# Eighty added pairs of fp32r products, with 128, 127 and 96 weight columns, between an up- and a down-projection

## The chip, the cores and the metric

The kernel runs on one core of a Trainium2 chip. The metric is the device time of one execution in microseconds (us), as a median of several. The core has five engines with a queue each: TensorE (PE in the profile) multiplies matrices, VectorE (DVE) and ScalarE (ACT) work on elements, GpSimd (POOL) does nearly nothing here, SyncE (SP) issues the loads. They meet at semaphores. A matmul holds one operand, the weights, in TensorE's array and streams the other, the moving operand, past it; the result goes to a bank of PSUM. The profile records two things for each: the load of the weights (LDWEIGHTS, on a row of its own, PEld) and the product (MATMUL).

## What is computed

Two transformer-like blocks on 256 tokens of width 2048, all inputs in float32. The part around the change is the feed-forward stage of the second block's first layer:

```python
def _conv_ffn(xn, w_up, conv_w, conv_b, w_down):
    up = xn @ w_up
    u, g = up[..., :D_FF], up[..., D_FF:]
    g = lax.conv_general_dilated(g, conv_w[:, None, :], ...) + conv_b
    return (jax.nn.silu(g) * u) @ w_down

for layer in range(2):
    ...                                   # attention, of another kind in each layer
    h = h + _conv_ffn(_rmsnorm(h, ffn_norm_g[layer]), ffn_w_up[layer], ...)
```

D_FF is 5632. Ahead of both layers stands a block with a gated recurrence and latent attention.

## The kernel before

**Products in two parts.** The large products are made from fp32r operands, a reduced form of float32. Each operand is split into a high part and a low part, so that a product is high x high + high x low + low x high. `pair` (line 647) makes them: for each of the 16 (or 22) blocks `k` of 128 rows and each of two output tiles `j` it issues two matmuls. The wide one holds 128 columns of the weights' high part and streams 512 columns, the high and the low part of the activations beside each other. The short one holds the low part of the weights and streams 256 columns. So a wide and a short product together, here called a couple (the change's own word for two such products is a pair), stream 768 columns. One call of `pair` over 16 blocks is 64 matmuls. The profile writes f32 for fp32r here as for plain float32; the products of line 647 are fp32r, all others with an f32 in their row are plain float32.

**The stage.** `ffn` runs twice, `ffn(False)` and `ffn(True)`. In it `g` goes over two halves of D_FF. In each half 22 calls of `pair` multiply the stream `xs` (128 partitions x 16 blocks x 512 columns, fp32r) with the weights of the up-projection, and then `residual_product(GROUP, ...)` multiplies the result, `ys` (22 blocks), with the weights of the down-projection in 8 calls of `pair`. In front of the down-projection's last two blocks TensorE waits for the last tiles of `ys` (semaphore `lo_out`), which VectorE finishes after the last up-projection's product.

**The supply of weights.** SyncE loads weights into `raw`, a ring of four slots of four blocks. ScalarE makes the high part in `wr` (line 1204), VectorE the low part (line 1654), TensorE waits for a slot (`unit_split`), and frees it (`unit_used`). So ScalarE, VectorE and the loads can be four slots ahead of TensorE, and no more.

**Banks.** `acc` is two pairs of banks, used in turn by `pair`; VectorE adds the two halves of a result when it reads it out (line 1665). `scores`, `turned`, `mixed` and `sums` are four more banks. `scores` is used by attention alone: in the first layer for the last time by `diff_scores`, after which ScalarE reads it (line 1353); in the second layer from `stick_scores` on. `T.scores_read` counts those reads.

**Addresses.** `xs` begins at 64 bytes past a multiple of 256, `wr` at 160 bytes past one (`MOVING_STEP`, `WEIGHTS_STEP`).

Each engine's order is that of its own code; nothing is moved by a scheduler.

Of the kernel before, what the change touches and what calls it, by code (L numbers as in the profile page):

```python
# [25 lines left out]
P = 128  # L26
TOK = 256
D = 2048
KT = D // P
# [195 lines left out]
def splits(units):  # L225

    return {f"unit_split{s}": units // RING for s in range(RING)}
# [58 lines left out]
def program(nc, t, out, consts):  # L286

    ctx = ExitStack()
    with ctx:
# [7 lines left out]
        def sb(name, shape, dt=F32):  # L297
            return ctx.enter_context(nc.sbuf_tensor(name, [P, *shape], dt))
# [39 lines left out]
        xs = sb("xs", [KT, 2 * TOK], F32R)  # L338
# [57 lines left out]
        scores = ctx.enter_context(nc.psum_tensor("scores", [P, 512], F32))  # L396
# [217 lines left out]
        def _(pe):  # L614
            T = Tallies(sems)
# [3 lines left out]
            def pair(right, blocks=KT, before=None, after=None, acc_wait=True, tokens_out=False):  # L619

                a = acc[pairs[0] % 2]
                if pairs[0] >= 2:
                    pe.wait_ge(*T.acc_read.next())
                else:
                    take(2 * pairs[0], 2 * pairs[0] + 1)
                pairs[0] += 1
                for n, k0 in enumerate(range(0, blocks, UK)):
                    s = units[0] % RING  # L630
                    units[0] += 1
                    pe.wait_ge(*T.unit_split[s].next())
                    for k in range(k0, min(k0 + UK, blocks)):
                        if before:
                            before(k)
                        w, x, first, last = wr[:, s, k - k0, :], right(k), k == 0, k == blocks - 1
                        for j in range(2):
                            cols = slice(j * P, j * P + P)
                            low = slice(256 + j * P, 256 + j * P + P)
                            if tokens_out:  # L640
                                wide = (a[:, j, :], x[:, cols], w)
                                short = (a[:, j, 0:256], x[:, low], w[:, 0:256])
                            else:
                                wide = (a[:, j, :], w[:, cols], x)
                                short = (a[:, j, 0:256], w[:, low], x[:, 0:TOK])
                            for ops in ((short, wide) if last else (wide, short)):
                                mm = pe.matmul(*ops, start=first and ops is wide, stop=last and ops is wide)  # L647
                    mm.then_inc(T.unit_used.sem, 1)
                    if after:
                        after(n)  # L650
# [155 lines left out]
            def take(*banks, read=None):  # L806

                for b in banks:
                    pe.wait_ge(*last_read[b])
                read = read or F.bank_read[banks[0]].next()  # L810
                for b in banks:
                    last_read[b] = read
                return bank(banks[0])
# [95 lines left out]
            for g in range(4):  # L909
                b = GA_BANK[g]  # L910
                take(b, b + 1)
                for u in range(4):
                    w = unit_tiles(one_unit())
                    for k in range(UK):
                        for j in range(2):
                            mm = pe.matmul(bank(b + j)[:, 0:TOK], w[:, k, j * P:(j + 1) * P], xm[:, u * UK + k, :],  # L916
                                           start=u == 0 and k == 0, stop=u == 3 and k == UK - 1)
# [32 lines left out]
            def stream_sums():  # L950

                T.squares_summed.n += KT // 2
                pe.wait_ge(T.squares_summed.sem, T.squares_summed.n)
                sums_bank()
                feature_sums(ssq, ones[:, :], sums[:, 0:TOK]).then_inc(T.sums_ready.sem, 1)
# [134 lines left out]
            residual_product(gates={0: 2, 12: 1, 14: 0}, meanwhile=last_head)  # L1090


            def ffn(last):
                ready = T.lo_out.n
                T.lo_out.n += KT // 2

                def normed_by(k):

                    if k % 2 == 0:
                        pe.wait_ge(T.lo_out.sem, ready + k // 2 + 1)  # L1100

                for g in range(2):
                    if g == 0:
                        pair(lambda k: xs[:, k, :], before=normed_by, after=lambda n: stream_sums() if n == 1 else None)
                        pair(lambda k: xs[:, k, :])
                    with T.turns(pe, GROUP // 2 - (g == 0), **splits(2 * UK), acc_read=2):
                        for e in range(2):
                            pair(lambda k: xs[:, k, :])
                    residual_product(GROUP, stored=g == 1 and last, tiles=1)

            ffn(False)


# [68 lines left out]

            residual_product(gates={0: 2, 12: 1, 14: 0}, meanwhile=last_heads)
            ffn(True)


# [1201 lines left out]
```

## Time and profile before

| | us |
|---|---|
| median of 3 runs | 2795.09 (2794.13 to 2795.55) |
| the profiled execution, whole | 2792.86 |
| its span, first to last instruction | 2791.1 |
| TensorE, busy with products | 2728.8 (98% of the span) |
| TensorE, busy with weight loads | 2374.5 (85%) |
| VectorE | 1983.0 (71%) |
| ScalarE | 1192.8 (43%) |
| DMA queue q1 (weights) | 523.60 MB, 62.1% of 16 engines' span |

Loads of weights overlap products, and the length of a product's record takes in its way through the array, which overlaps the next one. So the busy share of TensorE says that it never stands still, not at which pace it goes; the pace is read from the distance between starts.

### The profile page before, as it was taken

How to read it: one execution, taken by the hardware profiler on the slowest of the kernel's cores; microseconds unless marked ns; L12 is line 12 of the kernel's file. 1: busy time of each engine (PE TensorE's matmuls, PEld its weight loads, DVE VectorE, ACT ScalarE, POOL GpSimd, SP SyncE). 2: the span in 40 equal slices, each digit the busy share in tenths (PEclk: the TensorE clock that was granted, in tenths of full speed). 3: DMA queues.
4: the chain of work that ended last, by engine and by line, in shares of the span. 5: the costliest groups of instructions: out<-in, count | busy, mean ns of one | idle time of the engine just before them, and what ended most of it. 6: DMA issues, size and time to landing. Idle time of an engine off the chain costs nothing.

```text
span 2791.1 us, 43966 instructions
## 1 busy us (share of the span) xinstructions
PE 2728.8 (98%) x15236; PEld 2374.5 (85%) x15236; DVE 1983.0 (71%) x2617; ACT 1192.8 (43%) x1517; POOL 5.7 (0%) x12
## 2 busy tenths in 40 slices
PE   6899999999999999999999999999999999999999
PEld 5787888888878888888888888888888888888888
DVE  6555467777777777766777766588777775677765
ACT  1102444455544444444444443355444444444443
POOL 0000000000000000000000000000000000000000
PEclk9999999999999999999999999999999999999999
DMA  9886665555545666656666666643466666666664
GB/s 299 292 261 203 201 197 189 175 159 159 169 132 186 189 188 193 189 186 191 189 188 180 197 193 190 188 154 125 156 188 193 186 184 193 193 187 187 193 198 147
DMA packets 705761, 528.13 MB, mean 189 GB/s; under 512 B 32205, under 2 KB 694543, under 8 KB 705423
## 3 DMA queue, kind: packets, MB, share of 16 engines
q1 hardware_dynamic: 701728, 523.60, 62.1%
q10 hardware_dynamic: 3951, 3.44, 0.4%
q8 instruction: 51, 0.84, 0.1%
q14 instruction: 31, 0.25, 0.0%
HBM read 523.80 MB, written 2.10 MB: 188 GB/s over the span
## 4 chain that ended last, share of the span: by engine, by line
PE 91%; DVE 5%; issue 1%; ACT 1%; DMA 1%; ACTq 0%; SPq 0%; DVEq 0%
PE acc L647 78%; PE acc L727 2%; PE acc L715 2%; PE acc L916 2%; PE turned L727 1%; PE sums L727 1%; DVE pro_ada L1729 1%; DVE wr L1654 1%; PE sums L1031 1%; PE mixed L837 1%; DMA aring<-in_w_ada 1%; PE sums L655 0%; PE scores L1024 0%; ACT three_L L1589 0%; ACTq L1235 0%
## 5 line engine op out<-in xcount | busy, mean ns | idle before, releaser
L647 PE MATMUL acc<-xs,wr 128*128 128x512 f32 (+1 forms) x7680 | 1352.3, 337 | 0.2 <-DVE wr L1654 0.2
L647 PEld LDWEIGHTS acc<-xs,wr 128*128 128x128 f32 x7680 | 1174.4, 188 | 163.7 <-issue 3.8
L1654 DVE TENSOR_TENSOR wr<-raw,wr 128x1024 fp32r<-128x1024 f32 x832 | 1001.6, 1222 | 363.6 <-ACT wr L1204 351.6
L1204 ACT ACTIVATE wr<-raw 128x1024 fp32r<-128x1024 f32 x832 | 871.8, 1058 | 774.2 <-PE acc L647 767.5
L647 PE MATMUL acc<-ys,wr 128*128 128x512 f32 (+1 forms) x4352 | 762.5, 337 | 6.6 <-DVE ys L1688 6.6
L647 PEld LDWEIGHTS acc<-ys,wr 128*128 128x128 f32 x4352 | 666.5, 188 | 97.6 <-DVE ys L1688 6.4
L647 PE MATMUL acc<-wr,xs 128*128 128x512 f32 (+1 forms) x1024 | 183.3, 337 | 0.0
L647 PEld LDWEIGHTS acc<-wr,xs 128*128 128x128 f32 x1024 | 157.1, 188 | 23.0 <-issue 0.5
L1547 ACT ACTIVATE ffn_cv<-ffn_cv 128x256 f32<-128x256 f32 x88 | 36.9, 419 | 245.2 <-DVE ffn_cv L2241 245.2
L1665 DVE TENSOR_REDUCE ffn_ug<-acc 128x512 f32<-128x1024 f32 x88 | 107.8, 1224 | 39.6 <-PE acc L647 39.6
L1729 DVE SCALAR_TENSOR_TENSOR pro_ada<-aring,small,pro_ada 128x512 f32<-128x512 f32 (+1 forms) x112 | 92.4, 825 | 29.7 <-DMA aring<-in_w_ada 23.0
L1688 DVE TENSOR_TENSOR ys<-tmp,ys 128x256 f32 (+3 forms) x108 | 51.3, 475 | 73.2 <-ACT ys L1210 70.2
L1665 DVE TENSOR_REDUCE S<-acc 128x512 f32<-128x1024 f32 x72 | 87.9, 1220 | 21.3 <-PE acc L647 21.1
L1210 ACT ACTIVATE ys<-tmp 128x256 f32 (+3 forms) x104 | 46.8, 450 | 105.4 <-DVE tmp L2245 101.2
L715 PE MATMUL acc<-xm,w 128*128 128x256 f32 x256 | 64.0, 407 | 7.0 <-DVE xm L1747 6.1
L715 PEld LDWEIGHTS acc<-xm,w 128*128 128x128 f32 x256 | 52.0, 206 | 15.5 <-issue 6.4
L1669 DVE TENSOR_TENSOR ffn_ug<-ffn_ug,rx 128x512 f32<-128x512 f32 x88 | 60.8, 691 | 3.0
L916 PE MATMUL acc<-xm,w 128*128 128x256 f32 x256 | 57.3, 379 | 0.0
L916 PEld LDWEIGHTS acc<-xm,w 128*128 128x128 f32 x256 | 47.7, 190 | 6.0
L1286 ACT ACTIVATE sq<-acc 128x512 f32<-128x512 f32 x2 | 1.1, 594 | 119.6 <-PE scores L717 119.6
L2239 DVE SCALAR_TENSOR_TENSOR ffn_cv<-ffn_ug,vcol,ffn_cv 128x256 f32<-128x256 f32 x88 | 42.6, 484 | 13.2 <-DVE ffn_cv L2236 13.0
L2241 DVE SCALAR_TENSOR_TENSOR ffn_cv<-ffn_ug,vcol,ffn_cv 128x256 f32<-128x256 f32 x88 | 42.6, 485 | 13.0 <-DVE ffn_cv L2239 12.8
(306 smaller groups left out, 1505.2 us busy)
## 6 DMA issues: line engine op xcount, KB each, us to landing
raw<-in_ffn_w_up SPq DMA_DIRECT2D x704, 256.0 KB
raw<-in_ffn_w_down SPq DMA_DIRECT2D x160, 512.0 KB
raw<-in_a_w_qkv SPq DMA_DIRECT2D x96, 512.0 KB
raw<-in_b_w_kv SPq DMA_DIRECT2D x64, 512.0 KB
aring<-in_w_ada SPq DMA_DIRECT2D x96, 256.0 KB, 6.6
w<-in_w_in SPq DMA_DIRECT2D x48, 512.0 KB
raw<-in_w_ada SPq DMA_DIRECT2D x32, 512.0 KB, 5.7
raw<-in_w_out SPq DMA_DIRECT2D x32, 512.0 KB
```

The costliest lines, as they stand in the source:

```text
L647: mm = pe.matmul(*ops, start=first and ops is wide, stop=last and ops is wide)
L715: pe.matmul(bank(c // 2)[:, (c % 2) * TOK:(c % 2 + 1) * TOK], w[:, c * P:(c + 1) * P], xm[:, k, :], start=False, stop=k == KT - 1 and c % ...
L727: mm = pe.matmul(out(j), *here, start=k == 0, stop=k == UK - 1)
L916: mm = pe.matmul(bank(b + j)[:, 0:TOK], w[:, k, j * P:(j + 1) * P], xm[:, u * UK + k, :], start=u == 0 and k == 0, stop=u == 3 and k == UK ...
L1204: f(wr[:, s, :, 0:256], raw[:, s, :].rearrange("p (k n) -> p k n", k=UK), ACT.Copy)\
L1210: f(to[0], to[1], ACT.Copy).then_inc(T.hi_out.sem, 1)
L1654: tt(wr[:, s, :, 256:512], raw[:, s, :].rearrange("p (k n) -> p k n", k=UK), wr[:, s, :, 0:256], ALU.subtract).then_inc(T.unit_split[s].se ...
L1665: dve.tensor_reduce(out_tiles, a[:, 0:tiles, :].rearrange("p t (b c) -> p t c b", b=2), axis=AX_X, op=ALU.add)\
L1669: tt(out_tiles, out_tiles, both(rx), ALU.mult).then_inc(*T.acc_read.one())
L1688: tt(to[:, :, TOK:2 * TOK], src, to[:, :, 0:TOK], ALU.subtract).then_inc(*T.lo_out.one())
L1729: stt(here, aring[:, n % ADA_RING, 0:2 * kn * P], small[:, 8 + r:9 + r], here, ALU.mult, ALU.add)\
L2239: step(stt(cv[e][:, :], UG[e][:, 1, 1:1 + TOK], taps[1], cv[e][:, :], ALU.mult, ALU.add))
```

## The change

A new function `probe_products` is called once, on TensorE, in `ffn(False)` with `g == 0`: behind the 22 calls of the first up-projection and ahead of its down-projection. It waits until ScalarE has read the last `scores` of the first layer's attention, and then issues 160 fp32r matmuls, 80 of 512 and 80 of 256 moving columns, all into `scores`, each beginning a sum anew and ending it. Nobody reads what they leave. Both operands lie in `xs`: the moving one is block `k` from its first column on, the weights are 128, 127 or 96 columns of block `k + 1` from column 24 on, that is 160 bytes past a multiple of 256, as in `wr`. The five groups are:

| group | pairs | weight columns | rows | order of widths |
|---|---|---|---|---|
| A | 16 | 128 | 128 | 512, 256 |
| B | 16 | 127 | 128 | 512, 256 |
| C | 16 | 96 | 128 | 512, 256 |
| D | 16 | 128 | 127 | 512, 256 |
| E | 16 | 127 | 128 | 512, 512, 256, 256 |

```diff
+            def probe_products():
+
+                pe.wait_ge(T.scores_read.sem, T.scores_read.n + 1)
+
+                def once(k, cols, width, rows=P):
+                    pe.matmul(scores[0:cols, 0:width], xs[0:rows, (k + 1) % KT, 24:24 + cols], xs[0:rows, k, 0:width],
+                              start=True, stop=True)
+
+                for k in range(KT):
+                    once(k, P, 512)
+                    once(k, P, 256)
+                for k in range(KT):
+                    once(k, P - 1, 512)
+                    once(k, P - 1, 256)
+                for k in range(KT):
+                    once(k, 96, 512)
+                    once(k, 96, 256)
+                for k in range(KT):
+                    once(k, P, 512, rows=P - 1)
+                    once(k, P, 256, rows=P - 1)
+                for k in range(0, KT, 2):
+                    once(k, P - 1, 512)
+                    once(k + 1, P - 1, 512)
+                    once(k, P - 1, 256)
+                    once(k + 1, P - 1, 256)
+
             def ffn(last):
...
                         for e in range(2):
                             pair(lambda k: xs[:, k, :])
+                    if g == 0 and not last:
+                        probe_products()
                     residual_product(GROUP, stored=g == 1 and last, tiles=1)
```

On TensorE the loop of the up-projection was followed at once by the down-projection. Before:

```order
1834 L647 MATMUL acc<-xs,wr 128x256
1835 L647 MATMUL acc<-xs,wr 128x512
1836 L214 REGISTER_ALU
1837 L214 COMPARE_AND_BRANCH
1838 L647 MATMUL acc<-ys,wr 128x512
1839 L647 MATMUL acc<-ys,wr 128x256
```

Now the added products stand behind the loop's end (an order row gives the result's partitions and columns, so that 127x512 is a product with 127 weight columns):

```order
1835 L647 MATMUL acc<-xs,wr 128x512
1836 L214 REGISTER_ALU
1837 L214 COMPARE_AND_BRANCH
1838 L1098 MATMUL scores<-xs 128x512
1839 L1098 MATMUL scores<-xs 128x256
1840 L1098 MATMUL scores<-xs 128x512
1841 L1098 MATMUL scores<-xs 128x256
```

and the last of them, group E, ahead of the same first product of the down-projection:

```order
1978 L1098 MATMUL scores<-xs 127x512 x2
1979 L1098 MATMUL scores<-xs 127x256 x2
1980 L1098 MATMUL scores<-xs 127x512 x2
1981 L1098 MATMUL scores<-xs 127x256 x2
1982 L647 MATMUL acc<-ys,wr 128x512
1983 L647 MATMUL acc<-ys,wr 128x256
```

No other instruction is added, taken away or moved, on TensorE or on any other engine.

## Rows read from the trace of the kernel before

**Rows 1.** The page: busy time by engine, clock in 40 slices, chain by engine.
```profile
PE 2728.8 (98%) x15236; PEld 2374.5 (85%) x15236; DVE 1983.0 (71%) x2617; ACT 1192.8 (43%) x1517; POOL 5.7 (0%) x12
...
PEclk9999999999999999999999999999999999999999
...
PE 91%; DVE 5%; issue 1%; ACT 1%; DMA 1%; ACTq 0%; SPq 0%; DVEq 0%
```

**Rows 2.** Busy time by stretch: start:end length, then PE, PEld, DVE, ACT, POOL, clock, DMA.
```profile
1100.00:1150.00 50.00, 50.00 (x290) 44.02 (x289) 39.70 (x51) 20.77 (x26) 0.00 (x0) 1.00 0.68 197
1150.00:1200.00 50.00, 50.00 (x291) 44.02 (x289) 32.37 (x34) 22.54 (x24) 0.00 (x0) 1.00 0.60 187
...
1157.00:2791.10 1634.10, 1621.24 (x9357) 1425.43 (x9355) 1173.90 (x1445) 730.82 (x843) 0.00 (x0) 1.00 0.61 182
```

**Rows 3.** In order of time, around the place: start us, length us, engine, instruction, [idle].
```profile
1134.99 1.23 DVE L1665 TENSOR_REDUCE ffn_ug<-acc 128x512 f32<-128x1024 f32 x1 [0.46 <-PE acc L647]
...
1146.09 1.23 DVE L1665 TENSOR_REDUCE ffn_ug<-acc 128x512 f32<-128x1024 f32 x1 [0.45 <-PE acc L647]
...
1156.99 43.40 PE L647 MATMUL acc<-ys,wr 128*128 128x512 f32 x249
...
1157.19 1.23 DVE L1665 TENSOR_REDUCE ffn_ug<-acc 128x512 f32<-128x1024 f32 x1 [0.46 <-PE acc L647]
...
1163.30 0.43 DVE L1688 TENSOR_TENSOR ys<-tmp,ys 128x256 f32 x1 [0.81 <-ACT ys L1210]
```

**Rows 4.** In order of time, TensorE, four short looks at the up-projection.
```profile
999.86 0.51 PE L647 MATMUL acc<-xs,wr 128*128 128x512 f32 x2
...
1000.09 0.51 PE L647 MATMUL acc<-xs,wr 128*128 128x256 f32 x2
...
1000.21 0.51 PE L647 MATMUL acc<-xs,wr 128*128 128x512 f32 x2
...
1000.43 0.51 PE L647 MATMUL acc<-xs,wr 128*128 128x256 f32 x2
```

**Rows 5.** In order of time, TensorE, from the first block's end on.
```profile
399.62 3.62 PE L916 MATMUL acc<-xm,w 128*128 128x256 f32 x16
403.08 0.59 PE L837 MATMUL mixed<-one_pT,one_v 128*128 128x256 f32 x2
...
404.39 1.84 PE L866 MATMUL sums<-ones,gate_sum 128*128 128x1 f32 x16
407.02 89.04 PE L647 MATMUL acc<-ys,wr 128*128 128x512 f32 x512 [0.78 <-DVE ys L1688]
495.89 5.72 PE L647 MATMUL acc<-xs,wr 128*128 128x512 f32 x32
```

**Rows 6.** Groups by line and shape: count, busy us, mean ns of one, idle before.
```profile
L647 PEld LDWEIGHTS acc<-xs,wr 128*128 128x128 f32 x7680 | 1174.4, 188 | 163.7 <-issue 3.8 <-DVE wr L1654 0.5
...
L916 PEld LDWEIGHTS acc<-xm,w 128*128 128x128 f32 x256 | 47.7, 190 | 6.0
...
L1025 PEld LDWEIGHTS scores<-chunkb,identb 128*128 128x128 bf16 x32 | 3.1, 98 | 0.4
```

**Rows 7.** Last reads of scores ahead of the place: count, ns min/median/max, first to last start.
```profile
L1353 ACT ACTIVATION_READ_ACCUMULATOR two_p<-scores,small x4: 192/196/201, 816.3 to 819.7; 128x1 f32 x4
```

**Rows 8.** TensorE's waits, whole span: us in total, times, longest us; three of 18.
```profile
PE acc L647 <- DVE ys L1688: 6.6, 3, 3.4
...
PE mixed L1146 <- DVE three_A L2311: 4.9, 7, 1.7
...
PE turned L990 <- DVE ffn_fin L2100: 2.0, 1, 2.0
```

## The prediction

> **What bounds the kernel now.** I read the page first. TensorE is busy with products for 98% of the span, it makes up 91% of the chain of work that ended last, and its clock is granted in full in every slice [rows 1]; the stretches around the place show 1.00, the 2.4 GHz level [rows 2]. Then I asked for the place itself. In the two stretches of 50 us before and behind the end of the first up-projection TensorE is busy for 50.00 of 50.00 us, while VectorE is busy for 39.70 and 32.37 and ScalarE for 20.77 and 22.54 [rows 2]. The timeline shows the seam: the first product of the down-projection begins at 1156.99 with no idle time noted in front of it [rows 3]. The last tile of `ys` is done at 1163.30 + 0.43 = 1163.7, and the down-projection asks for it only in front of its last two blocks, 20 x 4 products behind its start, that is at 1156.99 + 80 x 0.1734 = 1170.9 (pace: below). So there is no wait at this seam that other work could fill. TensorE's own pace is all that counts here, and work put into its queue lengthens the chain by its whole length.
>
> **The pace of one product.** A call of `pair` is 64 matmuls, and VectorE reads its result when it is done: at 1134.99, 1146.09 and 1157.19 [rows 3]. That is 11.10 us each, so 11.10 / 64 = 173.4 ns for one, 346.9 ns for a wide and a short one. A far longer stretch agrees: 512 products from 407.02 to 495.89, 88.87 / 512 = 173.6 ns [rows 5]; the first quarter of these is written out without a loop, as the added ones are, and shows no gap. The starts tell the two widths apart: 999.86, 1000.09, 1000.21, 1000.43 [rows 4], so about 0.23 us for 512 columns and 0.12 for 256. Streaming alone at 2.4 GHz is 213.3 and 106.7 ns, so either has some 13 ns on top (26.9 ns by the better mean of a couple).
>
> **The weight loads.** There are as many loads as products in the whole trace, 15236 of either [rows 1], so 160 loads come with the 160 products. What does a load cost when nothing hides it? The products of one moving column show it: 16 of them take 1.84 us. The last one's record is 0.25 us long by the column of the row's end, so 15 distances take 1.59 us, 106 ns each [rows 5]. Behind a product of 256 columns, at 120 ns, such a load just disappears. Plain float32 products of 256 columns with as many weights come every (403.08 - 399.62) / 16 = 216 ns [rows 5], as long as 512 columns take to stream (213) and 3 ns: there the load is hidden whole. And is the load of an fp32r product of that kind? Its record is 188 ns long, a float32 one's 190, a bf16 one's 98 [rows 6]. I take it that it is: about 106 ns of loading behind an overhead common to all.
>
> **The change part by part.**
> 1. The wait on `scores_read`. ScalarE read `scores` for the last time at 819.7 + 0.2 [rows 7], 337 us before the place. It costs nothing, whatever the price of a semaphore that has long been passed; and nothing else is queued behind it that could have gone first.
> 2. Groups A and D, 32 pairs with 128 weight columns. Same widths, same starts of the operands within 256 bytes, same kind of operand as in `pair`. 32 x 346.9 ns = 11.1 us. That both operands lie in `xs`, that in D one row is missing, and that all results go to one bank instead of to two in turn, no row shows. A wide and its short product go to the same bank in the kernel too, at this pace, so I put nothing for it; my bound for either is the 13 ns on top of each product, gone or doubled, 160 x 13 ns = 2 us.
> 3. Groups B, C and E, 48 pairs with 127 or 96 weight columns. No row shows a load of fewer than 128 columns. From below: the load costs nothing at all and the 13 ns go with it, as in the float32 row: 96 x (13.4 - 2.7) ns = 1.0 us less. From above: it can't be hidden at all, 106 ns on each of the 64 products with 127 columns and 80 ns (three quarters) on each of the 32 with 96, 6.8 + 2.6 = 9.3 us more. I take the row nearest to it, the 128-column load of the same type: no more columns, no longer load, hidden as before. 48 x 346.9 ns = 16.7 us. The order in E (512, 512, 256, 256) puts a short product behind a short one; a load of 106 ns still fits into 120.
> 4. The other engines. Nothing is added to them. While TensorE is away for 28 us, ScalarE and VectorE fill the four slots of `wr` and SyncE those of `raw`, then they stand. That is lead which TensorE can't turn to time, since it waited for no weights here anyway [rows 2, 3]. The last results of the up-projection and `ys` are finished during the added work instead of during the down-projection; no wait depended on that either.
> 5. What comes later. All of TensorE's idle time behind 1157 is 1634.10 - 1621.24 = 12.9 us [rows 2], in waits for values that follow from its own results [rows 8]: `ys` at the start of later products, the sums of attention, the last transposes. A shift of everything by 28 us moves them along.
>
> The sum: 160 x 173.4 ns = 27.8 us. The profiled execution took 2792.86 us (its span of 2791.1 and 1.8 around it); with the change I expect 2820.6 there. The median of the runs is 2795.09, 2.2 us higher, so that the predicted median is 2795.09 + 27.75 = 2822.8 us, 1.0% more.
>
> **The rivals.**
> - *Narrow loads are of a slower kind.* Full columns might be loaded in a quick way that 127 and 96 columns don't get. What rows show as quick and slow is bf16 and float32, 98 and 190 ns, 92 apart [rows 6]. With that on top a narrow load takes 198 ns at 127 columns and 149 at 96. Behind a wide product (227 ns) it is still hidden, behind a short one (120) it stands out by 78 or 29 ns: 32 x 78 + 16 x 29 ns = 3.0 us more, 2825.8. Against it: the record of an fp32r load looks like the slow kind already. This is the rival that a rule of the Trainium skill speaks for, "TensorE: Matmul & The Clock Gate", Weight-path perf modes: fast weight load is on when there are 128 weights and the type isn't FP32, and reads the columns in four chunks side by side. By that rule with its theoretical factor of four an estimate would be 424 ns for a load of 127 columns and some 21 us more, 2843; the same page's section on LDWEIGHTS gives columns / 1.2 in ns, which is 107 at 128 (the trace agrees, 106), 106 at 127 and 80 at 96, and changes nothing.
> - *Narrow loads aren't hidden.* If the array can take new weights beside a running product only in full width, each narrow load stands in the open: 9.3 us more (step 3), 2832.2. For it: no row shows a narrow load hidden. Against it: the full-width load of either type is hidden in these rows, and a narrower one asks for less.
> - *Narrow products are cheaper.* 1.0 us less (step 3), 2821.8. It can't be told from my forecast by the time, only by the starts.
> - *Not slower.* The added work would have to fill time in which TensorE stands. The place for that is the wait for `ys` in the down-projection behind it, and the waits further on. At the seam the idle time is 0.0; giving back all 12.9 us of later idle time would still leave 14.9 us, so this decides only from 22 us of fillable idle time on, and the trace hasn't that. What is left of it is that the change doesn't do what it says: products whose result nobody reads are left out when the program is loaded, 2795.1. The built program holds all 160.
>
> **How the numbers follow.** My forecast (27.8 us, up or down by the 2 us of step 2) 0.68, cheaper narrow products 0.10, narrow loads of a slower kind 0.07 with 0.04 more for far slower ones (2843), narrow loads not hidden 0.09, not slower 0.02. The range from 2820.5 to 2833.0 leaves out the far slower loads, the last case and the odd ends. A difference of 0.2% (5.6 us) is about what a measurement of this kernel can tell from no change; every case but the last is well above it: slower 0.98, same 0.015, faster 0.005.
>
> **What would show it.** In the profile after: a group of 160 products into `scores`, in one stretch from about 1157 to 1184.7, with no idle time before, in or behind it, and the down-projection's first product at 1184.7. The stretch falls into five of 5.55 us each. If B, C and E are longer than A and D, the narrow load is the cause, and the starts say which way: some 80 ns more behind short products alone (a slower kind), or some 106 behind each (not hidden). If C is shorter than B, the load's length counts, so some of it isn't hidden. If A itself isn't 5.55, the fault is in the common step, the operands' place or the single bank. The forecast is wrong if the stretch isn't 27.8 us long within 2, or if the time behind it (1634 us before) changes by more than 1 us.

## The result, and the profile after

| | before | changed |
|---|---|---|
| median of the first 3 runs, us | 2795.09 (2794.13 to 2795.55) | 2820.67 (2819.98 to 2822.2) |
| the profiled execution, whole | 2792.86 | 2819.98 |
| its span | 2791.1 | 2817.9 |

The ratio is 1.0093, with a 95% interval of 1.007 to 1.0116: slower by 0.9%, by 25.6 us by these medians and by 27.1 us by the two profiled executions. The prediction was 2822.8 with a range of 2820.5 to 2833.0. In the experiments below one execution of the kernel before (5535.56 us) and one of idle9 (12833.07 us) were slow ones, which the ratios leave out.

The timeline of the changed kernel around the seam (start us, length us, engine, instruction, [idle]; the lines of the other engines are 28 higher than before, L1693 for L1665 and so on):

```profile
1156.18 1.22 DVE L1693 TENSOR_REDUCE ffn_ug<-acc 128x512 f32<-128x1024 f32 x1 [0.45 <-PE acc L647]
...
1155.98 28.00 PE L1098 MATMUL scores<-xs 128*128 128x512 f32 x160
...
1162.29 0.43 DVE L1716 TENSOR_TENSOR ys<-tmp,ys 128x256 f32 x1 [0.81 <-ACT ys L1238]
...
1183.82 6.41 PE L647 MATMUL acc<-ys,wr 128*128 128x512 f32 x36
1186.80 1.06 ACT L1232 ACTIVATE wr<-raw 128x1024 fp32r<-128x1024 f32 x1 [24.76 <-PE acc L647]
1187.89 1.23 DVE L1682 TENSOR_TENSOR wr<-raw,wr 128x1024 fp32r<-128x1024 f32 x1 [25.18 <-ACT wr L1232]
```

The 160 products stand in one piece, from 1155.98 to 1183.82, 27.84 us, with no idle time in front, inside or behind. ScalarE and VectorE finish the last tile of `ys` in its first quarter (1162.3 + 0.4), and then stand for 25 us: their four slots are full, and TensorE frees none. That lead is worth nothing later, as the busy time of the stretch behind the seam shows, here of the changed kernel (start:end length, PE, PEld, DVE, ACT, POOL, clock, DMA); the same stretch of before is the last of [rows 2]:

```profile
1183.80:2817.90 1634.10, 1621.27 (x9358) 1425.48 (x9356) 1169.23 (x1437) 729.16 (x840) 0.00 (x0) 1.00 0.61 181
```

1634.1 us in either kernel, with 1621.2 and 1621.3 us of products. Behind the seam nothing has changed to a tenth of a microsecond. Ahead of it the profiled execution of the changed kernel is 1.0 us early (1155.98 for 1156.99 in [rows 3]). That is the net of two differences. In the first block shorter waits (one for `pro_ada` took 3.3 us, 5.9 before) and a shorter stretch at half clock put it 3.1 us ahead (its first product of line 647 begins at 403.93, for 407.02 in [rows 5]), and then its clock was at half for a while where that of before stood at 1.00 (0.50 is the granted clock in this row of stretches):

```profile
404.70:408.10 3.40, 3.40 (x13) 2.92 (x12) 2.64 (x3) 2.66 (x3) 0.00 (x0) 0.50 0.81 250
```

That gave half of the lead back: the next products on `xs` begin at 494.38, for 495.89 before, 1.5 us ahead. These are differences between two executions, and no part of the change is there: 27.84 - 1.01 = 26.8 us is the difference of the spans.

The five groups can be told apart by their first products, each row from a short window of its own:

```profile
1155.98 0.39 PE L1098 MATMUL scores<-xs 128*128 128x512 f32 x1
...
1161.53 0.40 PE L1098 MATMUL scores<-xs 128*127 128x512 f32 x1
...
1167.12 0.39 PE L1098 MATMUL scores<-xs 128*96 128x512 f32 x1
...
1172.67 0.40 PE L1098 MATMUL scores<-xs 127*128 127x512 f32 x1
...
1178.24 0.39 PE L1098 MATMUL scores<-xs 128*127 128x512 f32 x1
...
1183.82 0.39 PE L647 MATMUL acc<-ys,wr 128*128 128x512 f32 x1
```

(128*127 in such a row is rows times columns of the weights.) So group A took 5.55 us, B 5.59, C 5.55, D 5.57 and E 5.58. Forecast were 5.55 for each. No longer run was made of D, so its 0.02 us may be chance. The records of the weight loads in this stretch (count, busy us, mean ns of one) do depend on the number of columns:

```profile
L1098 PEld LDWEIGHTS scores<-xs 128*127 128x127 f32 x64 | 9.8, 187 | 1.5
...
L1098 PEld LDWEIGHTS scores<-xs 128*128 128x128 f32 x32 | 5.0, 188 | 0.7
L1098 PEld LDWEIGHTS scores<-xs 127*128 127x128 f32 x32 | 4.9, 188 | 0.7
L1098 PEld LDWEIGHTS scores<-xs 128*96 128x96 f32 x32 | 4.5, 162 | 1.1
```

32 columns fewer make a load 26 ns shorter, 0.8 ns a column, and a product no faster: the load is hidden. A row fewer (127*128) leaves the record of the load at 188 ns.

### The profile page after: what moved, and what is told of

The parts are those of the page before. It is cut to its first block, busy times and chain, and to the rows that moved or that the text cites. A ratio compares the mean times of both kernels' runs of the same rounds, so it can differ in the third digit from the quotient of the medians.

```text
span 2817.9 us, 44286 instructions
## 1 busy us (share of the span) xinstructions
PE 2757.5 (98%) x15396; PEld 2399.2 (85%) x15396; DVE 1983.7 (70%) x2617; ACT 1193.1 (42%) x1517; POOL 5.7 (0%) x12
## 4 chain that ended last, share of the span: by engine, by line
PE 91%; DVE 5%; issue 1%; DMA 1%; ACT 1%; ACTq 0%; SPq 0%; DVEq 0%
PE acc L647 77%; PE acc L727 2%; PE acc L715 2%; PE acc L916 2%; PE turned L727 1%; PE sums L727 1%; DVE pro_ada L1757 1%; PE scores L1098 1%; DVE wr L1682 1%; PE sums L1031 1%; PE mixed L837 1%; DMA aring<-in_w_ada 0%; PE sums L655 0%; PE scores L1024 0%; ACTq L1263 0%
## 5 line engine op out<-in xcount | busy, mean ns | idle before, releaser
L1693 DVE TENSOR_REDUCE ffn_ug<-acc 128x512 f32<-128x1024 f32 x88 | 107.8, 1224 | 39.5 <-PE acc L647 39.5
L1693 DVE TENSOR_REDUCE S<-acc 128x512 f32<-128x1024 f32 x72 | 87.9, 1220 | 21.3 <-PE acc L647 21.1
L2269 DVE SCALAR_TENSOR_TENSOR ffn_cv<-ffn_ug,vcol,ffn_cv 128x256 f32<-128x256 f32 x88 | 42.7, 485 | 13.0 <-DVE ffn_cv L2267 12.8
```

The costliest lines, as they stand in the source:

```text
L1693: dve.tensor_reduce(out_tiles, a[:, 0:tiles, :].rearrange("p t (b c) -> p t c b", b=2), axis=AX_X, op=ALU.add)\
```

## The experiments

The experiments replace the body of `probe_products`, but for idle9. changed_again, eighty_full, full480, narrow480 and idle9 were executed several times; the others once, and they are read from their traces alone. In all of them the results in `scores` are read by nobody, as in the changed kernel. `mm(k, cols, width)` stands in the diffs for `pe.matmul(scores[0:cols, 0:width], xs[:, (k + 1) % KT, 24:24 + cols], xs[:, k % KT, 0:width], start=True, stop=True)`.

### Is it 27.8 us, and is it linear?

**changed_again** is the changed kernel, no edit. Expected:

> The changed kernel, timed again over five rounds beside the kernel before, since its first median was 25.6 us above and the forecast was 27.8. My theory (160 products at the pace of the kernel's own, 173.4 ns, nothing hidden): 27.8 us more, within 1.0 of it. A rival (some 2 us of the added work lie in idle time or are given back later): 25.6 again.

Measured: 2821.96 us against 2793.63 of before beside it, 28.3 us more, ratio 1.0102 (1.0085 to 1.0118). The rival of 2 us given back falls; 25.6 and 28.3 lie on either side of 27.8, and the medians of before themselves moved by 1.5 us between the two (its seven executions here lie between 2791.63 and 2797.18). In its trace the added products take 27.84 us once more.

**eighty_full**:

```diff
-                for k in range(KT):        # groups A to E
...
+                for k in range(80):
+                    mm(k, 128, 512)
+                    mm(k, 128, 256)
```

> 80 couples (a 512-wide and a 256-wide product) that all have 128 weight columns and 128 rows in place of the five groups. My theory: 80 x 346.9 ns = 27.8 us more than before, the stretch in the trace 27.8 us, so the same as the changed kernel but for its groups B and E, which showed 5.59 us in place of 5.55: 0.1 us less. Rival (narrow loads cost something that the groups' distances in the trace don't show): more than 0.5 us less than the changed kernel.

Measured: 2822.09 us, 28.5 us more, ratio 1.0102 (1.0086 to 1.0119): by the time the same as the changed kernel (0.1 us apart). Whatever the narrow weights cost, it can't be seen in the time of 80 couples. In the traces it can: the stretch is 27.74 us here (1155.63 to 1183.37) and 27.84 in the changed kernel, the 0.1 us that was expected.

**full480** and **narrow480** do it six times as long, with 128 and with 127 columns:

```diff
+                for k in range(480):
+                    mm(k, 128, 512)        # narrow480: 127
+                    mm(k, 128, 256)        # narrow480: 127
```

> 480 couples with 128 weight columns, six times the added work. My theory: 480 x 346.9 ns = 166.5 us more, in line with the 80. Rival (code written out without a loop runs short of instructions, or the engine's clock gives way): over 168. Rival (part of the added work is hidden): the increase isn't six times that of 80 couples, but some 2 us less than six times 27.8.

> 480 couples with 127 weight columns. By the distances of group B in the changed kernel (5.589 us for 16 couples against 5.551) 480 couples take 167.7 us where 128 columns take 166.5: 1.2 us more. Theory that narrow loads are hidden as wide ones and the 0.038 us are chance: the same as full480 within 0.5 us in the trace. Rival of unhidden loads: 102 us more, of a slower kind behind short products: 37 us more.

Measured: 2961.82 and 2961.47 us, 168.2 and 167.8 more than 2793.63, ratios 1.0601 (1.0583 to 1.0618) and 1.0599 (1.0582 to 1.0617). In the traces the stretches are exact. The first product of each, and the first product of the down-projection behind it, of full480:

```profile
1157.55 0.39 PE L1098 MATMUL scores<-xs 128*128 128x512 f32 x1
...
1323.95 0.39 PE L647 MATMUL acc<-ys,wr 128*128 128x512 f32 x1
```

and of narrow480:

```profile
1158.00 0.40 PE L1098 MATMUL scores<-xs 128*127 128x512 f32 x1
...
1325.47 0.74 PE L647 MATMUL acc<-ys,wr 128*128 128x512 f32 x3
```

166.40 us with 128 columns, 346.7 ns a couple, as forecast, and 167.47 us with 127, 1.07 us more. So the added work is linear, 960 products written out in a row don't run short of instructions, and nothing of it is hidden: the rival "2 us less than six times" would show some 164. By the letter the 168.2 us of full480's median lie over the 168 of the other rival, an engine short of instructions or of clock. The stretch itself, 166.4 us at a granted clock of 1.00, rules that out for the added work. But far behind the seam, after the 2.43 us in which TensorE waits for `ys` in the second layer, the clock of full480 was at half for 3.4 us, where before and narrow480 kept 1.00:

```profile
2136.60:2140.00 3.40, 3.40 (x13) 2.81 (x12) 3.40 (x4) 1.06 (x1) 0.00 (x0) 0.50 0.48 145
```

Its time behind the seam is 1635.9 us for 1634.1. Such a stretch, there in one execution and absent in the next, is part of what the medians scatter by; they don't show the 1.07 us between 128 and 127 columns. The 0.04 us by which group B was longer wasn't chance either: it is 2.2 ns a couple, 0.6%. It is far from what an unhidden load (102 us more here) or one of a slower kind (37 us) would cost.

### What would a load cost in the open?

**short_products** makes the product so short that it hides nothing:

```diff
+                for cols in (128, 127, 96, 64, 32):
+                    for k in range(32):
+                        mm(k, cols, 16)
+                for width in (64, 128, 256):
+                    for k in range(32):
+                        mm(k, 32, width)
```

> The added work is replaced by eight groups of 32 fp32r products each: 16 moving columns with 128, 127, 96, 64 and 32 weight columns, then 32 weight columns with 64, 128 and 256 moving columns. Nothing hides a load here. Theory (a load takes 0.83 ns a column, whatever the number of columns): distances of 106, 105, 80, 53 ns, and at 32 columns 27 or the floor of a product. Rival (only 128 columns load quickly, narrower ones in another way that the long products of the changed kernel hid): 127 columns clearly above 106. Then the last three groups: 64, 128, 256 moving columns at the engine's pace, 27 + 13, 53 + 13, 107 + 13 ns, if fp32r streams one column a cycle at any width; four times as long for the first two if it does not.

Measured: the timeline, one row for each group.

```profile
1158.16 4.40 PE L1098 MATMUL scores<-xs 128*128 128x16 f32 x32
1162.41 6.97 PE L1100 MATMUL scores<-xs 128*127 128x16 f32 x32
1169.23 5.27 PE L1102 MATMUL scores<-xs 128*96 128x16 f32 x32
1174.35 3.56 PE L1104 MATMUL scores<-xs 128*64 128x16 f32 x32
```

From start to start that is 4.25 / 32 = 133 ns for 128 columns, and then 6.82 / 32 = 213 ns for 127. Taken alone it looks like the rival, a load that is slower by over half with one column less. But the clock says otherwise (the number behind POOL's in a row of stretches):

```profile
1158.20:1160.80 2.60, 2.60 (x26) 2.60 (x24) 2.21 (x3) 1.06 (x1) 0.00 (x0) 1.00 0.89 273
1160.90:1162.40 1.50, 1.50 (x9) 1.50 (x9) 1.20 (x4) 0.17 (x1) 0.00 (x0) 0.50 0.24 85
1162.40:1169.20 6.80, 6.80 (x33) 6.80 (x34) 1.69 (x3) 0.66 (x2) 0.00 (x0) 0.50 0.24 77
```

With nothing but 16-column products TensorE was granted half its clock, the 1.2 GHz level, though it is busy for 6.80 of 6.80 us. It fell inside the group of 128 columns, so 133 ns is a mean of two paces, and the last seven of that group can be set against those of 127:

```profile
1160.91 1.64 PE L1098 MATMUL scores<-xs 128*128 128x16 f32 x7
```

(1162.41 - 1160.91) / 7 = 214 ns with 128 columns, and 213 with 127 at the same clock: the run does answer its question, against the rival. It also tells that at 1.2 GHz 213, 160, 107 and 53 ns for 127, 96, 64 and 32 columns are all two array cycles a column; and fp32r with 64 and 128 moving columns came every 53 and 106 ns, one column a cycle, so my "four times as long" in the expectation isn't so. (With 64 moving columns the load of 32 columns takes the same 53 ns.)

**short_clocked** puts 24 long couples ahead of each group of 16 short products:

```diff
+                for cols in (127, 128, 96, 64, 32):
+                    for k in range(24):
+                        mm(k, 128, 512)
+                        mm(k, 128, 256)
+                    for k in range(16):
+                        mm(k, cols, 16)
```

> Five groups of 16 fp32r products with 16 moving columns and 127, 128, 96, 64 and 32 weight columns, each behind 24 couples of long products, so that the granted clock can stay at 1.00; in short_products it was 0.50 to 0.54 from the second group on, so that its 213 ns for 127 columns against 112 for 128 told nothing. Theory (two array cycles a column at the granted clock and some 5 ns, for any number of columns): 127 columns 111 ns, 128 112, 96 85, 64 58, 32 some 32. Rival (128 columns load quicker): 127 columns clearly above 112, up to 213.

Measured: the clock is at 1.00 for the whole of it,

```profile
1156.40:1204.50 48.10, 48.10 (x322) 43.07 (x321) 5.20 (x8) 1.90 (x3) 0.00 (x0) 1.00 0.10 30
```

and the distances within the groups are 111, 112, 85, 58 and 32 ns for 127, 128, 96, 64 and 32 columns. The group with 127, and what follows it:

```profile
1164.81 1.81 PE L1101 MATMUL scores<-xs 128*127 128x16 f32 x15
1166.47 0.48 PE L1103 MATMUL scores<-xs 128*128 128x512 f32 x1
```

The group's first product begins at 1164.77 and the second, by this row, at 1164.81, only 31 ns later by the trace: at the head of such a group one distance is short. The 15 distances from the second product on take 1166.47 - 1164.81 = 1.66 us, 111 ns each. So a load of fp32r weights takes two cycles a column and 5 ns, for each of the five numbers of columns, and there is no quicker way for exactly 128. The rival "of a slower kind" falls for fp32r, not only by its price but by its mechanism.

**types** and **bf16_clocked** ask the same of the other two types. types has groups of bf16 products (weights from `identb`, moving operand from `chunkb`) and plain float32 ones (both from `h`), without long products between; bf16_clocked has the bf16 groups behind 24 long couples each.

```diff
+                # bf16_clocked; (cols, width):
+                for cols, width in ((127, 16), (128, 16), (126, 16), (96, 16), (64, 16), (127, 128), (128, 128)):
+                    for k in range(24):
+                        mm(k, 128, 512)
+                        mm(k, 128, 256)
+                    for k in range(16):
+                        pe.matmul(scores[0:cols, 0:width], identb[:, 0:cols], chunkb[:, 0:width], start=True, stop=True)
```

> The added work is replaced by groups of 32 bf16 products (weights from a 128-column identity, 16 moving columns) with 128, 127, 96, 64 and 32 weight columns, two groups of bf16 with 128 moving columns and 128 or 127 weight columns, and four groups of 16 plain float32 products: 256 moving columns with 128 and 96 weight columns, 16 moving columns with 128 and 96. For bf16 the quick load is to be seen if it hangs on the number of columns: 128 columns at the product's own floor (some 25 to 60 ns), 127 at up to 106 ns; if it does not hang on it, 127 as 128. For float32: two records of 216 ns a product at 256 columns with either width, and 106 against 80 ns a record at 16 columns.

> The same with bf16 products: 16 moving columns with 127, 128, 126, 96 and 64 weight columns, then 128 moving columns with 127 and 128, each behind 24 couples. In types 128 columns came every 25 ns and 127 every 59 at the full clock. Theory (bf16 has a quick load for exactly 128 columns): 59, 25, 58, 45 (96 / 2.4 + 5), 32, then 59 for 128 moving columns with 127 or 128 alike, or a little more where the load is the longer. Rival (the 25 ns were the start of the stretch): 128 columns as 127, some 59.

Measured: in bf16_clocked 59 ns for 127 columns, 25 for 128, 58 for 126, 45 for 96, 32 for 64, and with 128 moving columns 59 and 56 ns for 127 and 128. Two groups of it:

```profile
1166.30 1.06 PE L1101 MATMUL scores<-chunkb,identb 128*127 128x16 bf16 x16
...
1175.62 0.56 PE L1106 MATMUL scores<-chunkb,identb 128*128 128x16 bf16 x16
```

So the quick load for exactly 128 columns exists, for bf16: 25 ns against 59, and one column less loses it. As soon as the product is 128 columns long the loss is 3 ns of 56. In types the same: 128 columns every 25 ns, 127 every 59 at the full clock, before the clock fell to the 1.2 GHz level in this run too (1.00 in 1158.20:1160.80, 0.50 in 1161.20:1163.60). The plain float32 products gave 216 ns a record with 128 and with 96 weight columns at 256 moving columns, and 112 and 85 ns at 16: the same loads as fp32r, hidden in the same way.

### What are the 13 ns, and the 2?

The prediction carried 13 ns over the streaming in each product as part of the pace. In group A of the changed kernel it is 16 ns for the wide product (229.5 from start to start) and 11 for the short one (117.4). Three runs look at them.

**address** moves the weights' first column in steps of 8 (32 bytes), so where they lie to the moving operand within 256 bytes:

```diff
+                for at in (0, 8, 16, 24, 32, 40, 48, 56):
+                    for k in range(16):
+                        pe.matmul(scores[:, :], xs[:, (k + 1) % KT, at:at + 128], xs[:, k % KT, :], start=True, stop=True)
+                        pe.matmul(scores[:, 0:256], xs[:, (k + 1) % KT, at:at + 128], xs[:, k % KT, 0:256], start=True, stop=True)
```

> Eight groups of 16 couples with 128 weight columns, whose weights begin 0, 8, 16, 24, 32, 40, 48 and 56 columns behind the moving operand's place within 256 bytes (32 bytes a step); 24 is the changed kernel's and the kernel's own. It looks for the 13 ns that each product takes over its streaming. Theory A (they are fp32r's own or the load's hand-over): 5.55 us in every group. Theory B (they hang on where the two operands lie to each other): groups differ, and 24 is among the best.

**widths** has other numbers of weight columns:

```diff
+                for cols in (128, 127, 126, 124, 112, 96, 64, 32):
+                    for k in range(16):
+                        mm(k, cols, 512)
+                        mm(k, cols, 256)
```

> Eight groups of 16 couples as in the changed kernel with 128, 127, 126, 124, 112, 96, 64 and 32 weight columns. It looks for the 2 ns a couple by which 127 columns are slower (5.589 against 5.551 us in the changed kernel; 167.47 against 166.41 us over 480 couples), and for what a load of any length leaves in the open. Theory A (an odd number of columns costs it): 127 alone is at 5.59, all others at 5.55. Theory B (any number that isn't 128 or a multiple of 32): 126, 124 and 112 too. Theory C (the 13 ns on top of each product come with the length of the load): 64 and 32 columns well below 5.55, down to 5.33 at no load.

Measured, us for 16 couples, from the first product of a group to that of the next:

| address: first column | 0 | 8 | 16 | 24 | 32 | 40 | 48 | 56 |
|---|---|---|---|---|---|---|---|---|
| us | 5.64 | 5.65 | 5.64 | 5.56 | 5.62 | 5.61 | 5.65 | 5.56 |

| widths: weight columns | 128 | 127 | 126 | 124 | 112 | 96 | 64 | 32 |
|---|---|---|---|---|---|---|---|---|
| us | 5.55 | 5.59 | 5.60 | 5.64 | 5.55 | 5.55 | 5.55 | 5.58 |

The two rows that bound the group of 124 columns in widths:

```profile
1174.72 0.39 PE L1107 MATMUL scores<-xs 128*124 128x512 f32 x1
...
1180.37 0.39 PE L1110 MATMUL scores<-xs 128*112 128x512 f32 x1
```

The place matters, by up to 1.7% (5.65 against 5.56), and 24, which is the kernel's own distance, is one of the two best, as theory B had it; but at the best place the 13 ns are still there. In widths none of the three theories holds as written. It isn't the odd number (126 and 124 cost more than 127), nor any number that isn't a multiple of 32 (112 is free, 32 isn't), and not the load's length alone: with a quarter of the columns a couple is no faster. Short products in a row are, though. short_products, back at a clock of 1.00, has 256 moving columns with 32 weight columns:

```profile
1184.77 3.68 PE L1112 MATMUL scores<-xs 128*32 128x256 f32 x31
```

The next product begins at 1188.28, so that is 3.51 / 31 = 113 ns, 7 over the streaming, where 128 weight columns take 119 (streams, below). Part of the amount goes with the weights' columns there; which part is whose stays open. Why 124 columns cost 5.6 ns a couple and 112 none stays open. Since the place and the number of columns both change where the reading of the weights ends relative to the moving operand's, one cause for both is possible, but no run here shows it.

**streams** varies the moving columns, one width a group:

```diff
+                for width in (512, 448, 384, 320, 256, 192, 128):
+                    for k in range(32):
+                        mm(k, 128, width)
+                for k in range(16):        # plain float32
+                    pe.matmul(scores[:, 0:256], h[:, (k + 1) % KT, 24:24 + 128], h[:, k % KT, 0:256], start=True, stop=True)
```

> Groups of 32 fp32r products with 128 weight columns and 512, 448, 384, 320, 256, 192 and 128 moving columns, then 16 plain float32 ones with 256. It asks what the 13 ns over the streaming are that an fp32r product takes (in the changed kernel 229.5 ns where 512 columns stream in 213.3, 117.4 where 256 stream in 106.7). Theory A (one amount for each product): every group lies 13 ns above columns / 2.4, so 227, 200, 173, 147, 120. Theory B (5 ns for each and 5% of the streaming): 229.5, 201, 173, 145, 117.5. Both: the load of 106 + 5 ns bounds 192 and 128 moving columns at 112. Float32: 216 ns for each of its two records, 3 ns above its streaming.

Measured: the timeline of the groups.

```profile
1158.22 7.66 PE L1098 MATMUL scores<-xs 128*128 128x512 f32 x32
1165.72 6.57 PE L1100 MATMUL scores<-xs 128*128 128x448 f32 x32
1172.13 5.71 PE L1102 MATMUL scores<-xs 128*128 128x384 f32 x32
1177.67 4.85 PE L1104 MATMUL scores<-xs 128*128 128x320 f32 x32
1182.37 3.96 PE L1106 MATMUL scores<-xs 128*128 128x256 f32 x32
1186.16 3.71 PE L1108 MATMUL scores<-xs 128*128 128x192 f32 x32
1189.71 3.71 PE L1110 MATMUL scores<-xs 128*128 128x128 f32 x32
```

From start to start, divided by 32: 234, 200, 173, 147, 119, 111 and 111 ns. From 448 to 256 columns that is 12 to 14 ns over columns / 2.4, one amount for each product, as theory A had it. It doesn't hold at 512, where it is 21 when one wide product follows another (16 in the changed kernel, where a short one follows a wide one). Plain float32 stays at 3 ns over. And the last two show where the load takes over: with 192 moving columns, 80 ns of streaming, a product costs 111 ns, all of it the load's. In this kernel the short product (117 ns in a couple, 119 in a row of its kind) is just long enough to hide a load of 112, with 5 to 7 ns to spare.

### Would it have cost nothing elsewhere?

**idle9** adds nine couples (18 fp32r products whose results nobody reads) to the kernel before, at another place, and nothing at the seam. The expectation speaks of one such place. The edit has two: both attention layers call this function with `meanwhile`, and the trace holds 18 products of either width, half of them from 828.52 on and half from 1965.93 on.

```diff
                 def gated(k):
 
                     if meanwhile and k >= blocks - 3:
                         meanwhile(k)
+                    if meanwhile and k == 14:
+                        pe.wait_ge(T.scores_read.sem, T.scores_read.n + 1)
+                        for b in range(9):
+                            pe.matmul(scores[:, :], xs[:, b + 1, 24:24 + P], xs[:, b, :], start=True, stop=True)
+                            pe.matmul(scores[:, 0:256], xs[:, b + 1, 24:24 + P], xs[:, b, 0:256], start=True, stop=True)
                     if k in out:
                         pe.wait_ge(T.lo_out.sem, ready - out[k])
```

> The kernel before with nine couples (3.1 us) added at another place: in the residual product of the first attention layer, right ahead of the wait for the last tiles of ys, where TensorE stands for 3.4 us in the trace of before. Nothing is added at the seam. My theory (added work costs its length only where TensorE doesn't stand): the wait shrinks to about 0.3 us, and the time is as before, +0.0 to +0.3 us. Rival (the added work delays it anyway, since loads and semaphores around it count too): +3.1 us.

Measured: 2791.9 us against 2794.25, ratio 0.9992 (0.9983 to 1.0001), no slower. TensorE at the first place, before,

```profile
826.47 0.70 PE L1044 MATMUL sums<-sq,ones 128*128 128x256 f32 x2 [1.38 <-DVE sq L2164]
830.55 4.85 PE L647 MATMUL acc<-ys,wr 128*128 128x512 f32 x14 [3.38 <-DVE ys L1688]
```

and in idle9:

```profile
828.17 0.70 PE L1049 MATMUL sums<-sq,ones 128*128 128x256 f32 x2 [1.39 <-DVE sq L2169]
...
831.72 0.28 PE L985 MATMUL scores<-xs 128*128 128x256 f32 x1
832.27 3.97 PE L647 MATMUL acc<-ys,wr 128*128 128x512 f32 x21 [0.27 <-DVE ys L1693]
```

The wait went from 3.38 to 0.27 us, and the two groups of products stand 4.08 and 4.10 us apart: nine couples of 347 ns vanished in the wait. They even won time behind it. In a row of stretches each, first before and then idle9, with the products that follow the wait:

```profile
830.55:835.30 4.75, 4.75 (x15) 4.08 (x16) 4.72 (x5) 1.06 (x1) 0.00 (x0) 0.50 0.44 139
...
832.27:837.00 4.73, 4.73 (x27) 4.19 (x28) 4.70 (x5) 1.06 (x1) 0.00 (x0) 1.00 0.48 142
```

Before, TensorE had been busy for 0.70 of the 4.08 us ahead and its granted clock was at 0.50; in idle9 the added products kept it busy and the clock stayed at 1.00, so that 27 products stand where 15 did. In every other trace of this case the clock was at 0.50 there; the gain itself is read from one execution of idle9. VectorE's second read of the results behind the wait shows what it is worth, again first before and then idle9:

```profile
845.51 1.23 DVE L1665 TENSOR_REDUCE S<-acc 128x512 f32<-128x1024 f32 x1 [0.40 <-PE acc L647]
...
845.06 1.23 DVE L1670 TENSOR_REDUCE S<-acc 128x512 f32<-128x1024 f32 x1 [0.40 <-PE acc L647]
```

From the group in front of the wait (826.47 and 828.17) that is 19.04 and 16.89 us, 2.15 us less with the added work than without. At the second place the wait is shorter than nine couples. Before,

```profile
1966.27 0.38 PE L838 MATMUL mixed<-three_A,three_vcur 128*128 128x128 f32 x2
1969.09 6.17 PE L647 MATMUL acc<-ys,wr 128*128 128x512 f32 x34 [2.43 <-DVE ys L1688]
```

and in idle9:

```profile
1965.80 0.39 PE L838 MATMUL mixed<-three_A,three_vcur 128*128 128x128 f32 x2
...
1969.16 6.06 PE L647 MATMUL acc<-ys,wr 128*128 128x512 f32 x34
```

2.82 us have become 3.36: the wait is filled, and 0.54 us of the nine couples stand in the open. Here the clock was at 1.00 in either kernel, and nothing is won. Both places together give 1.6 us less; the medians say 2.4 us less, with an interval that doesn't leave out no change. So the cost of added products is set by where they stand: 347 ns a couple at the seam, where TensorE never waits, nothing inside a wait, and the excess over the wait where they are longer than it.

## Why the prediction was right, point by point

- *What bounds the kernel.* Right. No wait at the seam, and the 1634.1 us behind it are the same in both traces, with 12.8 us of idle time for 12.9. The four slots of lead were worth nothing. But "its clock is granted in full in every slice" reads means of 70 us: before, the clock was at 0.50 for the first products behind the wait at 830.55 (above). None of that lies at the seam, so the forecast didn't suffer.
- *The pace.* Right: 346.9 ns a couple were forecast from calls of `pair`; 346.7 came out over 480 couples. All results in one bank, and both operands in `xs`, cost nothing that is seen. The 13 ns "on either" are 16 and 11; the forecast used their sum alone, and that was right.
- *Step 2, groups A and D.* 11.1 us forecast, 5.55 + 5.57 = 11.12 measured.
- *Step 3, groups B, C and E.* 16.7 us forecast, 5.59 + 5.55 + 5.58 = 16.72 measured. The row taken as nearest, the full-width load of the same type, was the right one. Its price in the open was read wrong, though: 106 ns from the one-column products, where fp32r itself gave 111 to 112. The 5 ns were in the trace of before already:

```profile
404.42 1.81 PE L866 MATMUL sums<-ones,gate_sum 128*128 128x1 f32 x15
```

The second of the 16 products begins 0.03 us behind the first (404.39), and the 14 distances from it on take 1.81 - 0.25 = 1.56 us, 111 ns each. I had averaged the short first distance with the others. It matters: behind a short product the load has 5 to 7 ns to spare, not 14. And a small term was missed, 2 ns a couple with 127 columns, 0.07 us in groups B and E.
- *The sum.* 27.8 us forecast, 27.84 in the trace. The profiled execution was to take 2820.6 us and took 2820.0, since it was 1.0 us early at the seam. The median was to be 2822.8; it was 2820.67 in the first runs and 2821.96 in the next ones. The difference to the forecast is the spread of the executions, which the range allowed for only just: its lower end, 2820.5, was 2.3 us below the forecast, and the lowest of the first three executions lay under it.
- *Narrow loads of a slower kind.* Falls. The rule of the Trainium skill behind it ("TensorE: Matmul & The Clock Gate", Weight-path perf modes) does hold on this chip for bf16: 25 ns for 128 columns, 59 for 127. For fp32r, which isn't named there, 112 and 111 ns show no quick load to lose. The factor of four, from which the prediction worked out its 424 ns, is given there as theory for fp8; bf16 shows 25 against 59 ns. Its other rule, columns / 1.2 in ns (section LDWEIGHTS), gives 107 for 128 columns. The prediction's "the trace agrees, 106" rests on the mean above: fp32r and float32 take 112 at the full clock, 5 ns more than the rule. bf16 without the quick load takes half of the rule and 5 ns (59 ns for 127), and at the 1.2 GHz level fp32r takes twice (213 ns).
- *Narrow loads not hidden.* Falls: that would have made group C 2.6 us longer and B 3.4, and over 480 couples 102 us. C took 5.55 us, B 5.59, and the 480 couples 1.07 us more.
- *Narrow products cheaper.* Falls for couples as in the change: 96 columns took 5.55 us like 128, and 32 columns 5.58. In a row of short products alone 32 columns took 113 ns for 119, so that the 13 ns aren't wholly apart from the load.
- *Not slower.* Not here. idle9 shows the mechanism at the places where it works.

## What to carry to other kernels

Work added to the engine that bounds a kernel costs its own pace where that engine never waits, and nothing where it stands, up to the length of the wait; so read the idle time in front of the very instruction that will follow, not the engine's share of the span. Whether a property of the weight load (its type, its number of columns) can be seen at all depends on how long the product in front of it is: compare the load's time in the open (here 112 ns for 128 columns of a four-byte type) with the product's. And look at the granted clock before reading any small test of TensorE: a row of tiny products lowered it, and doubled every number. Look at it behind a wait too, in stretches as short as the wait: work that fills one can keep the clock up for what follows (2.15 us won at the first place of idle9). And in a group of short products leave the first distance out of the mean, or it hides some ns of each.

## What I had not expected of the hardware

- fp32r and float32 load weights in two cycles a column and 5 ns (112, 111, 85, 58, 32 ns for 128, 127, 96, 64, 32 columns); bf16 in one cycle a column and 5 ns, but for exactly 128 columns, where products come every 25 ns.
- 16-column products in a row, with TensorE busy for all of the time, brought the granted clock to 0.50 (short_products: 1.00 in 1158.20:1160.80, 0.50 in 1160.90:1162.40); with 24 long couples between groups of 16 it stayed at 1.00.
- Behind the wait at 830.55 the granted clock was 0.50 before, and 1.00 when the wait was filled with products; behind the 2.43 us wait of the second layer it was 1.00 before and 0.50 in full480, with the same code there.
- With 128 weight columns and products of one width in a row, an fp32r product of 256 to 448 moving columns takes 12 to 14 ns over its streaming, where plain float32 takes 3; at 512 columns it is 21 (16 in a couple), at 256 with 32 weight columns 7. Where it comes from is open.
- The place of the weights within 256 bytes to that of the moving operand is worth up to 1.7% of fp32r products' time, and 127, 126 or 124 weight columns cost 0.6 to 1.7%, where 112, 96 and 64 cost nothing.
